# A two-block transformer layer in one kernel: the order and the size of the first transfers

## What is computed

```python
def hybrid_layer(x, c, w_ada, b_ada, norm_g, w_in, ...):
    mod = (jax.nn.silu(c) @ w_ada + b_ada)[:, None, :]
    shift, scale, gate = jnp.split(mod, 3, axis=-1)
    h = rms_norm(x, norm_g) * (1.0 + scale) + shift
    (a_q, a_kv, ..., d_z) = jnp.split(h @ w_in, IN_OFFSETS, axis=-1)
    # four attention-like branches over h, each gated and projected, then summed
    ...
    return x + gate * (merged @ w_out)
```

## Time and profile before

| | us |
|---|---|
| median of 3 runs | 2966.54 (2966.51 to 2966.85) |
| profiled execution, its own time | 2968.03 |
| span of its trace | 2966.3 |
| TensorE matmuls busy | 2697.6 (91% of the span) |
| VectorE, ScalarE, GpSimd busy | 949.6, 932.4, 878.7 |
| mean granted TensorE clock | 0.942 of full speed |

### The profile page before, as it was taken

How to read it: one execution, slowest core, us unless ns; L and a number is a source line. 1 busy time by engine, 2 the same in 40 slices (tenths; PEclk the granted TensorE clock), 3 DMA queues, 4 the chain that set the end, 5 groups by cost and what they waited for, 6 DMA issues and landing times.

```text
span 2966.3 us, 29752 instructions
## 1 busy us (share of the span) xinstructions
PE 2697.6 (91%) x12244; PEld 2125.0 (72%) x12244; DVE 949.6 (32%) x1423; ACT 932.4 (31%) x1308; POOL 878.7 (30%) x497
## 2 busy tenths in 40 slices
PE   4799999999998999999988999696999999999696
PEld 2677778666687777788777777473888888888475
DVE  6212440233202454511237564406022222222512
ACT  3102441688721344421332333223211111112221
POOL 1212111343321111133642121243333322334343
PEclk9888999999997899999989999898999999999798
DMA  6101011100011000011221000110111111111011
GB/s 266 43 22 41 27 33 43 36 18 18 15 50 42 18 19 10 15 44 42 100 74 62 15 29 27 54 67 8 50 50 50 43 50 50 50 50 43 32 45 66
DMA packets 33431, 134.81 MB, mean 45 GB/s; under 512 B 3536, under 2 KB 3856, under 8 KB 32400
## 3 DMA queue, kind: packets, MB, share of 16 engines
q1 hardware_dynamic: 32976, 131.85, 12.7%
q10 hardware_dynamic: 320, 1.05, 0.1%
HBM read 123.45 MB, written 8.39 MB: 44 GB/s over the span
## 4 chain that ended last, share of the span: by engine, by line
PE 79%; DVE 9%; POOL 4%; ACT 3%; issue 3%; DMA 1%; SPq 0%; POOLq 0%; ACTq 0%; DVEq 0%
PE slot L613 48%; PE slot L658 12%; PE ps L826 4%; PE ps L797 3%; DVE mm L1612 2%; PE ps L775 2%; PE ps L859 1%; PE ps L850 1%; POOL wlo L1432 1%; PE ps L863 1%; PE ps L876 1%; DVE cacc L2015 1%; POOL xlo L1439 1%; DMA mm<-xT 1%; POOL pbuf L1446 1%
## 5 line engine op out<-in xcount | busy, mean ns | idle before, releaser
L613 PE MATMUL slot<-xhi,whi 128*128 128x512 f32 x2192 | 720.5, 411 | 95.8 <-DVE xlo L1764 32.9
L613 PE MATMUL slot<-xlo,whi 128*128 128x512 f32 x2192 | 693.8, 398 | 0.0
L613 PE MATMUL slot<-xhi,wlo 128*128 128x512 f32 x2192 | 690.2, 397 | 0.0
L1432 POOL TENSOR_TENSOR wlo<-raw,whi 128x1024 fp32r<-128x1024 f32 (+1 forms) x169 | 427.7, 2531 | 766.5 <-ACT whi L1070 766.5
L613 PEld LDWEIGHTS slot<-xhi,whi 128*128 128x128 f32 x2192 | 407.4, 194 | 196.0 <-issue 83.7
L613 PEld LDWEIGHTS slot<-xlo,whi 128*128 128x128 f32 x2192 | 423.3, 193 | 92.9
L613 PEld LDWEIGHTS slot<-xhi,wlo 128*128 128x128 f32 x2192 | 421.5, 192 | 92.4
L1070 ACT ACTIVATE whi<-raw 128x1024 fp32r<-128x1024 f32 (+1 forms) x169 | 185.9, 1100 | 276.4 <-PE slot L658 174.5
L658 PE MATMUL slot<-uhi,whi 128*128 128x512 f32 x512 | 158.3, 390 | 0.0
L658 PE MATMUL slot<-ulo,whi 128*128 128x512 f32 x512 | 157.8, 389 | 0.0
L658 PE MATMUL slot<-uhi,wlo 128*128 128x512 f32 x512 | 157.6, 389 | 0.0
(11 more groups left out here) (301 smaller groups left out, 3223.0 us busy)
## 6 DMA issues: line engine op xcount, KB each, us to landing
raw<-wstream SPq DMA_DIRECT2D x129, 512.0 KB, 3.2
raw<-wstream SPq DMA_DIRECT2D x40, 640.0 KB, 3.8
ada<-wada SPq DMA_DIRECT2D x6, 2048.0 KB, 30.3
mm<-xT SPq DMA_DIRECT2D x1, 4096.0 KB, 24.0
mm<-xT SPq DMA_DIRECT2D x8, 512.0 KB, 3.8
res_dram<-mm SPq DMA_DIRECT2D x8, 512.0 KB, 6.2
res<-res_dram SPq DMA_DIRECT2D x8, 512.0 KB, 6.6
outT<-res SPq DMA_DIRECT2D x8, 512.0 KB, 2.6
```

Source lines behind the costliest of these rows:

```text
L613: o = mm_(outs[:, half * HALF:(half + 1) * HALF], w[b % 2][:, k_w, :], x[:, k_x, half * HALF:(half + 1) * HALF], start=first and j == 0, s ...
L1432: tt(flat(wlo[b % 2])[:, 0:n], raw[:, 0:n], flat(whi[b % 2])[:, 0:n].bitcast(F32), ALU.subtract).then_inc(w_lo, 1)
```

## The change

The loads at the beginning change order and size. `vec` stays first. `tab` is laid out anew, with what is used early in front (identity, ones, small constants: 294 columns), and only that part comes second. x follows in two halves of 2 MB with a semaphore each. Then `ada1` and `ada0` come in eight pieces of 512 KB each, one for each row chunk, and each product waits for its own piece. The rest of `tab` (2176 columns) comes behind the first weight block. VectorE's casts of the tables and the negation of `sink` move behind norm1, with a wait for the rest of `tab`. The order of `ada1` before `ada0` stays, and so does what TensorE and GpSimd do.

```diff
-    for name, n in [("dist", S), ("ident", P), ("strict", P), ("tri", P), ("negones", P), ("ones", P),
-                    ("up", P), ("low", P), ("cdist", NB * NCMP), ("cmask", NB * NCMP), ("gc", 2),
-                    ("eps6", 1), ("eps5", 1), ("invw", 2), ("invc", 32)]:
+    for name, n in [("ident", P), ("ones", P), ("gc", 2), ("eps6", 1), ("eps5", 1), ("invw", 2), ("invc", 32),
+                    ("strict", P), ("tri", P), ("negones", P), ("up", P), ("low", P), ("cdist", NB * NCMP),
+                    ("cmask", NB * NCMP), ("dist", S)]:
...
+EARLY = TABLES["strict"][0]
...
             sp.dma_start(vec[:], vecs).then_inc(small_in, 16)
-            sp.dma_start(tab[:], tables).then_inc(small_in, 16)
+            sp.dma_start(tab[:, 0:EARLY], tables[:, 0:EARLY]).then_inc(small_in, 16)
             for half in range(2):
-                sp.dma_start(ada1[:, 4 * half:4 * half + 4, :], wada[1][:, 4 * half:4 * half + 4, :]
-                             ).then_inc(ada_in[1][half], 16)
-            sp.dma_start(mm[:], xT).then_inc(x_in, 16)
-            for half in range(2):
-                sp.dma_start(ada0[:, 4 * half:4 * half + 4, :], wada[0][:, 4 * half:4 * half + 4, :]
-                             ).then_inc(ada_in[0][half], 16)
+                sp.dma_start(mm[:, 4 * half:4 * half + 4, :], xT[:, 4 * half:4 * half + 4, :]).then_inc(x_in[half], 16)
+            for t, a in ((1, ada1), (0, ada0)):
+                for kc in range(8):
+                    sp.dma_start(a[:, kc, :], wada[t][:, kc, :]).then_inc(ada_in[t][kc], 16)
...
             load_weights(0)
+            sp.dma_start(tab[:, EARLY:NTABLE], tables[:, EARLY:NTABLE]).then_inc(tab_in, 16)
             sp.dma_start(rtab[:], rtables).then_inc(rtab_in, 16)
...
-            act.wait_ge(x_in, 16)
             for n in range(NC):
+                if n % 4 == 0:
+                    act.wait_ge(x_in[n // 4], 16)
                 chunk_square(0, n, mm[:, n, :])
...
             dve.wait_ge(small_in, 32)
-            link(v.tensor_copy(identb[:], t_("ident")))
-            link(v.tensor_copy(upb[:], t_("up")))
-            link(v.tensor_copy(lowb[:], t_("low")))
             link(v.memset(token[:], 1.0))
-            v.tensor_scalar(nsink[:], v_("sink"), -1.0, None, ALU.mult).then_inc(masks_done, 1)
...
-                ada_products(t, [[(slice(0, D), a[:, kc, :], kc // 4)] for kc in range(8)])
+                ada_products(t, [[(slice(0, D), a[:, kc, :], kc)] for kc in range(8)])
...
                     applied(0, x_src, 8)
+                    dve.wait_ge(tab_in, 16)
+                    link(v.tensor_copy(identb[:], t_("ident")))
+                    link(v.tensor_copy(upb[:], t_("up")))
+                    link(v.tensor_copy(lowb[:], t_("low")))
+                    v.tensor_scalar(nsink[:], v_("sink"), -1.0, None, ALU.mult).then_inc(masks_done, 1)
```

More of the change, by code:

```diff
@@ L427, in build @@
         res_dram = nc.dram_tensor("res_dram", [P, NC, S], F32, kind="Internal").ap()
-        small_in, x_in, raw_in, rtab_in = (sem(n) for n in ("small_in", "x_in", "raw_in", "rtab_in"))
-        ada_in = [[sem("ada_in%d%d" % (i, half)) for half in range(2)] for i in range(3)]
+        small_in, tab_in, raw_in, rtab_in = (sem(n) for n in ("small_in", "tab_in", "raw_in", "rtab_in"))
+        x_in = [sem("x_in%d" % half) for half in range(2)]
+        ada_in = [[sem("ada_in%d%d" % (i, part)) for part in range((8, 8, 2)[i])] for i in range(3)]
         xres_in = [sem("xres_in%d" % n) for n in range(NC)]
```

## The result

| | before | after |
|---|---|---|
| first 3 runs of before, as known ahead | 2966.54 (2966.51 to 2966.85) | |
| median of 10 runs each, us | 2967.56 (2966.51 to 2972.22) | 2975.61 (2974.22 to 2977.48) |
| ratio, 95% interval | | 1.0023 [1.0014, 1.0032] |
| span of the profiled execution | 2966.3 | 2975.7 |

The changed kernel is slower by 0.23%; the prediction had 2968.2 and a range up to 2970.0. Two things came together. The start lost 2.3 us, by the mechanism of the prediction. Another 7.1 us of the two profiled executions are lost 1.7 ms later, in a stage that the change does not touch.

The account below looks back on a forecast made before the run. TensorE ends the chain for 79% of the span, and all hangs on the square sums at the start. +1.7 us from their later start, 0 from the clock, 0 from the rest, on 2966.54: 2968.2 us, range 2965.6 to 2970.0.

Parts of the forecast that it names:

- TensorE's own order, which the change leaves alone: Kernel start: square sums stay behind ada1's small matmuls, so start at 29.5 us against 27.79, +1.7 us (+0.4 to +2.3).
- the ends given for the clock: Square sums at the start: slow-clock time between 2.05 us won back and 0.9 lost; no change, 16.04 us, taken.
- the fast rival: Kernel start: square sums run as x lands, reciprocal at 39.3 to 41 us, -5.5 to -7 us, about 2960; chance 4%.
- Hidden parts: Start: earlier ada0, first block, rest of tab, extra issues and moved casts are covered by other work; 0 us.
- the rival of pieces that don't overlap: Weight loads at the start: each 512 KB piece pays 3.2 us in turn, sums 17 us later, 2983.7 us; chance 5%.
- The rival of slower table reads: TensorE's 176 weight loads from tri and negones: 25 ns more each costs 4.4 us, a doubling 33 us (3001); chance 3%.
- 0 from the rest: Term of the sum: everything apart from the square sums' start and the clock adds 0 us.
- Two waits for ScalarE on halves of x are met long before: ScalarE's squares at the start: the waits for x's two halves were taken to cost nothing.
- The base: The shift was added to the median of the kernel before, 2966.54 us.
- the start's bounds: Range from the start: low end +0.4 - 2.05, taken as -0.9 (2965.6); high end +2.3 + 0.9 and 0.3 for runs (2970.0).
- a shift is a shift of the whole kernel: From the square sums on: moving their start or end moves everything behind equally, here 1.7 us, if the order holds.

Follow-up runs that it names:

- e3: Changed kernel with TensorE's square sums put ahead of the modulation of the first weights: 2967.8 us, 0.9993 of before.
- e7: Changed kernel with TensorE's square sums ahead of the first weights' modulation and a single ScalarE wait for x: 2962.6 us, 0.9977 of before.
- e1: Kernel before with only the new table layout and the late casts, transfers in their old order and sizes: 2972.8 us, 1.0006 of before.
- e6: Kernel before with one more ScalarE wait on x, ahead of the fifth square and long met: 2974.0 us, 1.0015 of before.
- e8: The changed kernel itself measured once more, nothing altered: 2974.7 us, 1.0018 of before.
- e5: Changed kernel with both halves of x on one semaphore and a single ScalarE wait: 2972.2 us, 1.0008 of before.
- e2: Kernel before with two useless VectorE operations ahead of the four small operations near 45 us: 2971.4 us, 1.0009 of before.
- e9: Changed kernel with three useless VectorE operations of 0.2 us each in norm2, at about 1515 us: 2971.0 us, 1.0007 of before.
- e14: Kernel before with a ScalarE wait on x added mid-kernel, ahead of branch C's weight split near 470 us: 2971.9 us, 0.9998 of before.

## Why the prediction was wrong

- **The start: right mechanism, nearly the right size.** The step "TensorE's own order, which the change leaves alone" held: the wait for x became one for ada1's products. Products ended at 26.1 (25.8 forecast), the small matmuls took 3.54, the sums began at 29.8 (29.5), and ran 16.3 us (16.04), as six of them were slow, for 5.1 us, instead of five for 4.1; that lies within the ends given for the clock. The reciprocal came at 48.53 (47.9). In all +2.3 instead of +1.7 us. e3 and e7 confirm it from the other side: with that order turned, the start moves from 2.3 us late to 5.4 us early, which is the fast rival's at its small end (its own terms add up to -5.2 to -6.9, not -5.5 to -7).
- **Hidden parts: right.** ada0's products ended at 36.4, first block, rest of tab and casts cost nothing at the start, and the pieces came at the pace of VectorE (0.48 us of waiting in eight): the rival of pieces that don't overlap fell. The rival of slower table reads fell with e1. VectorE idled 11.5 us ahead of the small operations, not about 8: the prediction's own times (products to 37, TensorE's sums to 47.2) give 10. The loads ahead of the second block are 25, not 24. Neither touches the sum. SyncE stood still in its issues of ada pieces (18 us for sixteen) without harm.
- **"0 from the rest": this is the step that failed.** I took "Two waits for ScalarE on halves of x are met long before" as free, looking for time at the wait. What the runs showed in its place: the wait costs by being there. It is one instruction more in a stream, puts a delay of 0.28 us on one copy 1 ms later, and from there the work meets the clock differently. By the pairs measured (e6 against before, e8 against e5) it is worth 2.5 to 5.2 us in the median, and 7.1 us between the two profiled executions, where the kernel before stood well. In the forecast it was 0, and no rival held it.
- **The base.** The forecast stood on the three runs shown, 2966.5 to 2966.9. The kernel's own spread is 2965 to 2975 and more, its median 2969.1. I read the narrow three as precision. A range made of the start's bounds alone was then too narrow even for the kernel before.
- **"a shift is a shift of the whole kernel"** does not hold run by run: e2 delayed the start by 2.2 us and its median came 1.2 us later, and in the trace of e5 a lag of 2.7 us behind before at 77 us was gone at 334 us.

## What to carry to other kernels

Look where an early load's consumer stands in its engine's own order: bringing x forward gained nothing while TensorE had the products of other data ahead of it, and turning two lines there (with one wait for x instead of two) put the kernel 0.2 to 0.3% under the one before. Where a kernel has stages in which TensorE's clock comes and goes, compare versions by the starts of the same instruction through the whole trace, and by many runs: a difference of a few us far from the edit may come from where the work meets the clock, and a useless instruction can bring it (e6) or take it away (e9). Three close runs are no measure of such a kernel's spread.

## What the runs showed of the hardware

- A stage in which TensorE partly waits can take one of a few lengths, not a smear: the piece of 573 matmuls took 115.9 to 116.5 us, 119.2 to 119.4, or 122.0 to 123.1, with a granted clock of 0.97, 0.94 and 0.90 to 0.91. Which one it took went in all 18 traces with where the work ahead of it lay against the clock's fall (3.6 to 3.7, 5.4 to 6.0, 4.1 to 4.2 us): with 0.6 us of delay 4.18 became 3.59 and 123.07 became 116.54.
- A wait that is long met still costs where it takes an instruction of its own: a third semaphore on an instruction that had two added none (e14), a second on one that had one added one (e6). With that one instruction a copy 1 ms later was 0.28 us late in six traces of six, and with two or three it was not. The late instruction is the 832nd of ScalarE's stream there and the 1088th in before, each with a load of instructions starting 0.63 to 0.66 us behind it; whether the fetching is the cause stays open.
- The pages' granted clock reads 1.00 from the start although the first square sums take nearly double time (1054 ns mean for the first six of after's and 1056 for the first five of before's, against 602 behind them); the durations are the better witness there.
